# Half as many loaded chunks, twice as many split weight blocks, in a two-block transformer on one core

## The reference, cut to what matters

```python
mod = c_act @ ada_w[layer] + ada_b[layer]          # six rows of 2048
u = rms_norm(h, norm_mix_g) * (1.0 + sc1) + sh1
h = h + g1 * hybrid_mixer(u, w_in, ..., w_out)     # fox, nsa, dilated, diff
u = rms_norm(h, norm_ffn_g) * (1.0 + sc2) + sh2
h = h + g2 * swiglu(u, w_gate, w_up, w_down)
x = rms_norm(h, final_norm_g)
for i in range(2):                                 # the second block
    u = h @ w_in_2[i]; branch = pool(u) or moba(u, h @ w_kv_shared)
    mem_o = memory_attention(u, mem, w_mem_kv[i])
    h = layer_norm(ALPHA * h + mixed @ w_out_2[i], ln_g[i], ln_b[i])
```

## Time and profile before

| what | value |
|---|---|
| median of 3 runs | 2108.17 us (2106.98 to 2109.46) |
| profiled execution, its own time | 2107.47 us |
| its span, first to last instruction | 2105.8 us |
| mean granted TensorE clock | 0.997 of full speed |
| PE busy / DVE busy / ACT busy | 2063.4 / 1428.9 / 1064.1 us |
| read from HBM | 465.13 MB, 222 GB/s over the span |

### The profile page before, as it was taken

One profiled execution on the slowest core, in us unless ns is written; L12 is line 12 of the kernel. 1 busy time (PEld: TensorE's weight loads), 2 busy tenths in 40 slices (PEclk: granted clock), 3 DMA queues, 4 the chain that ended last, 5 costly groups with the idle time before them and its releaser, 6 DMA issues.

```text
span 2105.8 us, 28605 instructions
## 1 busy us (share of the span) xinstructions
PE 2063.4 (98%) x9837; PEld 1701.6 (81%) x9837; DVE 1428.9 (68%) x2490; ACT 1064.1 (51%) x1969; POOL 89.3 (4%) x159
## 2 busy tenths in 40 slices
PE   6999999999999999999999999999999999999997
PEld 5787788888877888888888888888788788888885
DVE  5987899899688885655555556854466655555556
ACT  3644555556454444445444454553455555555553
POOL 2001011010003000000000000100000000000000
PEclk9999999999999999999999999999999999999999
DMA  8999889888658886666666666664466556655562
GB/s 312 376 369 329 277 296 300 283 287 283 209 173 276 289 290 210 197 190 189 189 189 193 190 190 188 196 226 142 149 205 208 164 152 180 172 165 165 182 227 100
DMA packets 281610, 468.88 MB, mean 223 GB/s; under 512 B 17136, under 2 KB 111568, under 8 KB 280080
## 3 DMA queue, kind: packets, MB, share of 16 engines
q1 hardware_dynamic: 278720, 451.32, 66.6%
q0 software_dynamic: 2768, 15.98, 2.3%
HBM read 465.13 MB, written 2.10 MB: 222 GB/s over the span
## 4 chain that ended last, share of the span: by engine, by line
PE 93%; DVE 5%; issue 1%; DMA 0%; ACT 0%; SPq 0%; POOL 0%; DVEq 0%; ACTq 0%
PE ps L585 82%; PE ps L923 1%; DVE w_lo L530 1%; PE ps L895 1%; DVE acc_a L510 1%; PE ps L1489 1%; PE ps L1772 1%; PE ps L1123 1%; PE ps L1101 1%; PE ps L561 1%; PE ps L907 1%; DMA raw<-in_w_mem_kv 0%; PE ps L1674 0%; DVE ada_acc L542 0%; PE ps L1758 0%
## 5 line engine op out<-in xcount | busy, mean ns | idle before, releaser
L530 DVE TENSOR_TENSOR w_lo<-raw,w_hi 128x512 fp32r<-128x512 f32 (+1 forms) x1288 | 876.4, 691 | 617.6 <-ACT w_hi L482 613.1
L482 ACT ACTIVATE w_hi<-raw 128x512 fp32r<-128x512 f32 (+1 forms) x1288 | 804.5, 629 | 904.4 <-PE ps L585 867.3
L585 PE MATMUL ps<-w_hi,actT 128*128 128x512 f32 (+2 forms) x3712 | 1010.9, 394 | 0.0
L585 PEld LDWEIGHTS ps<-w_hi,actT 128*128 128x128 f32 x3712 | 684.8, 188 | 144.2 <-issue 10.0
L585 PE MATMUL ps<-w_lo,actT 128*128 128x512 f32 (+2 forms) x1856 | 571.1, 388 | 4.3 <-DVE w_lo L530 4.2
L585 PEld LDWEIGHTS ps<-w_lo,actT 128*128 128x128 f32 x1856 | 347.1, 188 | 80.2 <-DVE w_lo L530 7.4
L585 PE MATMUL ps<-w_hi,hidT 128*128 128x512 f32 x704 | 189.6, 391 | 0.0
L585 PEld LDWEIGHTS ps<-w_hi,hidT 128*128 128x128 f32 x704 | 131.4, 188 | 27.4 <-issue 0.5
L585 PE MATMUL ps<-w_hi,mixT 128*128 128x512 f32 x480 | 130.0, 390 | 0.0
L585 PE MATMUL ps<-w_lo,hidT 128*128 128x512 f32 x352 | 108.6, 390 | 0.5 <-DVE w_lo L530 0.5
L585 PEld LDWEIGHTS ps<-w_hi,mixT 128*128 128x128 f32 x480 | 89.8, 188 | 18.4
(11 more groups left out here) (309 smaller groups left out, 1461.0 us busy)
## 6 DMA issues: line engine op xcount, KB each, us to landing
raw<-in_w_in SPq DMA_DIRECT2D x208, 512.0 KB, 4.8
raw<-in_ada_w SPq DMA_DIRECT2D x192, 512.0 KB, 5.4
raw<-in_w_out SPq DMA_DIRECT2D x96, 512.0 KB, 4.1
raw<-in_ffn_w_gate SPq DMA_DIRECT2D x176, 256.0 KB, 2.9
raw<-in_ffn_w_up SPq DMA_DIRECT2D x176, 256.0 KB, 3.1
raw<-in_ffn_w_down SPq DMA_DIRECT2D x88, 512.0 KB, 4.1
raw<-in_w_kv_shared SPq DMA_DIRECT2D x48, 512.0 KB, 3.7
raw<-in_w_mem_kv SPq DMA_DIRECT2D x32, 512.0 KB, 7.0
```

Source lines behind the costliest of these rows:

```text
L482: act.activation(half(p, at_p, it.g + b, 0, w), raw[:, slot_of(st, it), b, 0:w], ACT.Copy).then_inc(hi_ready, 1)
L530: nc.vector.tensor_tensor(half(p, at_p, it.g + b, 1, w), raw[:, slot, b, 0:w], half(p, at_p, it.g + b, 0, w).bitcast(f32), ALU.subtract).t ...
L585: last = nc.tensor.matmul(ps[:, bank_of(st, it.j) + t, 0:w], lhs[:, int(which == 1), kk, t * P:(t + 1) * P], half(p, at_p, it.g + b, int(w ...
```

## The change

The two constants that set the lengths of the rings are changed. A loaded chunk takes 4 KB of a partition and a split block 4 KB (2 KB for each half), so the two rings together take the 48 KB that they took: 32 + 16 KB before, 16 + 32 KB now.

```diff
@@ -53,7 +53,7 @@
 ALPHA = 4 ** 0.25
 BR, MEMW, HD2 = 1536, 512, 128
 POOL_WINDOWS = (2, 4, 8, 16)
-RING, HILO = 8, 4
+RING, HILO = 4, 8
```

## The result

| | before | after |
|---|---|---|
| median of 4 runs, us | 2108.82 (2106.98 to 2110.04) | 2185.52 (2182.95 to 2186.77) |
| ratio, 95% interval | | 1.0363 (1.0351 to 1.0376) |
| span of the profiled execution, us | 2105.8 | 2183.0 |
| granted TensorE clock, mean | 0.997 | 0.986 |

The change makes the kernel 77 us slower. The forecast was 2133 us, with a range up to 2168, so the sign was right, and the forecast had a third of the loss.

What follows compares the result with a forecast made beforehand. The prediction took PE to set the time, with loads able to only in the first third. Its terms 16 + 10 + 2 + 0 - 3 = +25 us gave 2133 us, range 2106 to 2168.

Steps and rivals of the forecast that it cites:

- Removed slots, the size of the round: Four slots give one chunk per (landing + hold) / 4, with landing 4.8 us (3.6 to 5.7) and mean hold 1.65.
- Step 1: 16 to 187 us, `memkv` and `win_k`: 112 chunks at 1.61 us plus 5.5 for `x`; 16 us lost (0 to 42).
- The chain that the prediction named: End of `win_k`: DVE's eleven ada chunks end at 185.7 us and pass straight to PE's last sum; about 200 forecast.
- Step 2: 187 to 500 us, `win`: ring suffices on the mean, but uneven attention steps of DVE cost 10 us (0 to 25).
- Step 3: `gu0`: panels with ada chunks fall 3 us behind, the split ring covers it in the next; 2 us (0 to 8).
- Step 4: All stages with w chunks only: a round of 5.8 us against 10.7 us of PE's work; nothing lost.
- What the change adds: Longer split ring lets ACT and DVE run further ahead where PE ran dry: -3 us (0 to -7).
- the two dry spots of PE: PE ran dry for 1.2 us at 55 us and 1.6 us at 220 us, where it could gain.
- B: Four slots suffice: landing stays at 4.0 us or less, nothing lost in `memkv` and `win_k`; 2107 us, chance 0.12.
- C: Faster: landing under 4.0 us and eight split blocks keep PE from running dry; 2101 us, chance 0.08.
- D: Short ring costs much more: landing stays 5.7 us, 42 us lost up to 187 us, 25 in `win`; 2177 us, chance 0.15.
- The signs: Profile after: landing about 4.8 us, 330 to 345 GB/s early, ACT waiting for chunks, DVE idle above 37 us in `win`.

Runs made afterwards that it cites:

- steps ahead: Kernel after, with ACT's and DVE's attached steps in `win` and `wout` moved from between a w chunk's two blocks to ahead of it: 2165.5 us.
- four and four: Kernel after with the split ring left at 4 blocks, so 4 loaded chunks and 4 split blocks: 2195.6 us.
- lighter loads: Kernel after with each ada chunk loading only half its bytes, which DVE reads twice: 2134.7 us; the same edit on the kernel before: 2106.9 us.

## Why the prediction was wrong, by its own steps

**What bounds.** Right: the loads in the first third, PE in the rest. All of the loss arises before 820 us.

**Removed slots, the size of the round.** This is the step that failed, in one of its terms. The prediction put the round as "the landing time plus the hold", the hold as the bare instructions, 1.65 us on the mean. The landing was nearly right (4.8 forecast, 4.9 to 5.1 as the stages' means). What it lacked is that a slot is also taken while its chunk lies loaded and while the engines pause between its blocks: lying plus reading are 2.18 us in `memkv` and 3.17 in `win` on the mean, by the table above. The ada chunk lies there until DVE has the w chunk ahead of it behind it, 0.8 and 1.5 us; one of the two engines on a chunk waits for the other; in `win` attention steps stand between. These could be read before the change: between the two copies of a w chunk of `win` ACT works 49.1 us on L941 and 12.9 on L932, summed over the 72 chunks, in the trace of the kernel before as in that of the kernel after. The whole hold there, 4.6 us for a w chunk of `win`, could not be carried over as it stands, since it has waits for PE in it.

**Step 1**, 16 forecast, 28.7 measured. By the round, 64 chunks at 1.83 and 48 at 1.68 us make 198 us, where 181 + 5.5 was forecast. Against 4.8 + 1.65, lying and reading are worth 9.5 us more over these chunks, and the landing, 5.1 and 5.0 as means, 7.4; the 5.5 us put in apart for `x` stand against that. DVE's last ada sums and PE's sum behind them in the kernel after the earlier trace rows:

```profile
195.61 11.42 SPq L409 DMA_DIRECT2D raw<-in_ada_w  x8
198.40 11.78 PE L1489 MATMUL ps<-cmask,ident 128*128 128x384 f32 x36
201.97 1.28 DVE L510 SCALAR_TENSOR_TENSOR acc_b<-raw,c_col,acc_b 128x1024 f32<-128x1024 f32 x1 [0.73 <-DMA raw<-in_ada_w]
210.38 2.70 DVE L510 SCALAR_TENSOR_TENSOR acc_b<-raw,c_col,acc_b 128x1024 f32<-128x1024 f32 x2 [0.72 <-DMA raw<-in_ada_w]
213.14 3.15 PE L561 MATMUL ps<-ones,acc_b 128*128 128x1 f32 x14 [2.96 <-DVE acc_b L510]
```

The chain that the prediction named does end the part: the last sum starts at 213.14 instead of 185.83. DVE, which ran its eleven ada chunks without a gap before, now waits up to 0.73 us for chunks.

**Step 2**, 10 forecast, 33.8 measured, above even its end of 25. The step said that "on the mean the ring holds out, with 8% over". It doesn't: the round is 8.0 us and not 6.8, four chunks want 7.4. Here all of the miss is lying and reading, as the landing of 4.9 us is under the 5.1 that the step used. The steps ahead show the part of the pause between the reads: in their trace 18.6 of the 33.8 us go with it. The 4.1 us between 500 and 620 us, where `wout` begins with eight ada chunks, stand in no step.

**Step 3**, 2 forecast, 11.7 in the stretch to 820 us. "The split ring covers it in the next panel" was wrong in size. By DVE's last reads a mixed panel takes 28.5 to 29.3 us in the kernel after, where it took 24.2 to 26.2, so that it falls behind by 3 to 5 us; the panel without ada chunks behind it takes 18.7 to 19.9 us where it took 19.2 to 21.9, and gives back 0 to 3. The median of 4.5 us in this step was over loads of two sizes: in `gu0` a w chunk comes as two loads of 256 KB, an ada chunk as one of 512.

**Step 4** was right, 0: -0.3 us over 540.

**What the change adds**, -3 forecast. The sign was right, and four and four is 10 us slower than four and eight, but the place was not the two dry spots of PE: 7 of the 10 us go while the load of `x` holds up the chunks. Step 4 had such a cover in mind, "where a transfer of another queue holds a load up", but for the stages without ada chunks.

**The rivals.** B and C are refuted; the landing is not 4.0 us. D named nearly the right time, 2177 us, by a wrong mechanism, and by luck: with the landing at 5.7 us it had 42 us for step 1, where 28.7 came, and 25 for step 2, where 33.8 came. The Trainium skill, page "DMA: Bandwidth & Descriptors", section "Anatomy of one DMA — SWDGE (gpsimd) path", gives about 2.0 us and the bytes at 436 GB/s, an estimate of 3.2 us for 512 KB and 2.6 for 256 KB; the traces disagree for these loads, with medians of 4.8 and 3.5 us at some three in flight. The fit is for loads issued by GpSimd, and these are SP's.

**The signs.** ACT's waits for chunks, the median landing, DVE's idle time in `win` (65 us) and the part behind 820 us came as the prediction said. Two did not, and both for the slower round: 295 to 310 GB/s in the second to fourth slice and not 330 to 345, and the run of eleven ends at 213 us and not at about 200.

**What stays open.** First, the clock. Up to 2100 us PE ran at the lower of its two levels, 1.2 GHz, for 51 us in the kernel after and for 3.4 before (at the very end each has 11 to 13 us more); four matmuls take 2.07 us there (at 353.54 above) where they take 1.07 at the full one (at 1500.32 in the kernel before). In that case the clock had fallen at 349.5 us, behind this gap in PE's work:

```profile
349.37 2.65 PE L923 MATMUL ps<-proj,probsT 128*128 128x64 f32 x12 [2.71 <-ACT qkT L932]
```

The Trainium skill, page "TensorE: Matmul & The Clock Gate", section "HAM oscillation — how this bites in real kernels", has it that waits for loads between groups of matmuls drop the clock. The trace agrees in kind, but the longer gaps at the falls are waits for ACT or DVE (2.71 us here, 3.09 at 293.9), which come late themselves.

The clock's share of the 77 us was not separated. It is between nothing, if PE waits for chunks anyway, and half of the 48 us, 24. Two things on record say that it is the smaller part. The kernel before ran 22 times beside the last four kernels: at a mean clock of 0.998 it took 2106.9 us, at 0.994 and 0.995 2109.2, so 2.3 us for some 7 us of clock time lost. At that rate, which is an estimate from another kernel, the 24 us would cost some 8. And one run of the steps ahead took 2161.6 us at a mean clock of 0.990, 24 us less than the kernel after at 0.985 to 0.988, though by the clock it lost only 8 us less (another took 2169.4 at 0.991). Nor are the holds longer under the low clock: w chunks of `win` whose round meets it in the kernel after are held 3.29 us (18 of them), the others 3.33 (54). So the gain of the steps ahead is not the clock's in the main; a part of it may be.

Second, why a load takes 4.8 to 5.1 us in this ring, and not 4.2 or 3.8, was not taken apart further than by the lighter loads.

## What to carry to other kernels

A slot of a ring is taken from the issue of its load to the last read: landing, lying and reading, each as a mean over all kinds of chunk that share the ring, from the trace and not from the bare durations of the instructions. Divide by the slots and compare with the pace that is wanted; a chunk that lies loaded for some us before it is read is the margin, and where that is less than what the lost slots give, every further us in the hold costs a quarter of one per chunk with four slots. Look for work that stands between the first and the last read of a chunk: it costs nothing while the ring is deep, and 20 us here when it is short. And a large load of another queue can hold up all chunks for as long as it runs, here 10 to 12 us: with eight loaded chunks or eight split blocks PE got through it, with four of each it stood for 5 us.

## What was not expected of the hardware

Landing times went with the number of slots, and so of loads in flight: medians of 4.8 to 4.9, 5.3 and 6.0 us with four, five and six slots, and 5.7 to 6.7 with eight, for the same 512 KB. And a 512 KB load landed 0.5 to 0.8 us sooner, as the stages' means, when the ada chunks beside it had 256 KB, though the DMA engines were busy only 0.81 to 0.93 of the time in those stages before.
